# Hybrid encoder step: the overflow experts and the final combination move into the experts' block, and semaphores count from zero

## The reference

```
mod = silu(c) @ w_ada + b_ada                       # six rows of 1024 for each group
h = rms_norm(x, norm_mix) * (1 + sc1) + sh1
m = token_mixer(h, ...)                             # HGRN2 and GLA, chunked recurrences
    # merged = sigmoid(ga) * (o_hg @ w_br_a) + sigmoid(gb) * (o_gla @ w_br_b); m = merged @ w_out
x2 = x + g1 * m
h2 = rms_norm(x2, norm_ffn) * (1 + sc2) + sh2
# 32 experts (4 groups of 8), 2 chosen for each token with weights wts
y = sum over the two chosen experts: wts * ((silu(h2 @ w_gate[e]) * (h2 @ w_up[e])) @ w_down[e])
x3 = x2 + g2 * y
out = rms_norm(x3, norm_final)                      # and the new recurrent states
```

## Time and profile before

| | |
|---|---|
| median of 3 runs | 1918.81 us (1918.67 to 1918.93) |
| the profiled execution | 1918.63 us |
| its span in the profile | 1916.8 us |
| mean granted PE clock | 0.924 |
| busy: PE, DVE, ACT, POOL | 1617.3, 1274.5, 953.3, 323.6 us |
| instructions | 26572 |

### The profile page before, as it was taken

How to read it: one execution, slowest core, us unless ns; L and a number is a source line. 1 busy time by engine, 2 the same in 40 slices (tenths; PEclk the granted TensorE clock), 3 DMA queues, 4 the chain that set the end, 5 groups by cost and what they waited for, 6 DMA issues and landing times. The chain is left out here.

```text
span 1916.8 us, 26572 instructions
## 1 busy us (share of the span) xinstructions
PE 1617.3 (84%) x10704; PEld 1413.7 (74%) x10704; DVE 1274.5 (66%) x1507; ACT 953.3 (50%) x1159; POOL 323.6 (17%) x186
## 2 busy tenths in 40 slices
PE   4579999999899998985696996499999999999800
PEld 2459989988789898984696785388888888887600
DVE  2534368267658575855454436789999999998727
ACT  2724234332625353443102211478888888888623
POOL 0100001000101010100220000134442332322113
PEclk8789999999999999998698998699999999999955
DMA  8722101201111202111542534699999999999546
GB/s 337 292 57 68 35 12 64 88 25 35 60 47 36 70 23 73 34 51 52 182 137 90 201 121 136 234 344 370 377 376 382 378 360 372 367 371 373 200 177 234
DMA packets 189073, 347.06 MB, mean 181 GB/s; under 512 B 18290, under 2 KB 74202, under 8 KB 187868
## 3 DMA queue, kind: packets, MB, share of 16 engines
q1 hardware_dynamic: 171676, 308.48, 45.4%
q10 hardware_dynamic: 7392, 19.06, 2.6%
q0 software_dynamic: 9888, 17.88, 2.5%
HBM read 316.71 MB, written 44.38 MB: 188 GB/s over the span
## 5 line engine op out<-in xcount | busy, mean ns | idle before, releaser
L133 PE MATMUL x_psum_proj<-h_hi,x_w_hi 128*128 128x364 f32 (+1 forms) x1056 | 362.7, 343 | 23.6 <-ACT x_v L652 11.8
L134 PE MATMUL x_psum_proj<-h_lo,x_w_hi 128*128 128x364 f32 (+1 forms) x1056 | 351.3, 333 | 0.0
L135 PE MATMUL x_psum_proj<-h_hi,x_w_lo 128*128 128x364 f32 (+1 forms) x1056 | 351.0, 332 | 0.0
L133 PEld LDWEIGHTS x_psum_proj<-h_hi,x_w_hi 128*128 128x128 f32 x1056 | 202.1, 191 | 32.5 <-ACT x_v L652 12.7
L134 PEld LDWEIGHTS x_psum_proj<-h_lo,x_w_hi 128*128 128x128 f32 x1056 | 202.4, 192 | 2.3
L135 PEld LDWEIGHTS x_psum_proj<-h_hi,x_w_lo 128*128 128x128 f32 x1056 | 202.1, 191 | 0.0
L510 POOL CAST x_w_hi<-x_w 128x1024 fp32r<-128x1024 f32 x44 | 73.1, 1661 | 664.6 <-PE x_psum_proj L135 662.2
L1751 POOL DMA_INDIRECT scratch_y<-e_y,all_tbl x32 | 79.6, 2486 | 392.3 <-ACT e_y L1825 367.8
L1006 DVE TENSOR_REDUCE x_sc<-x_diag 64x64 f32<-64x448 f32 x136 | 126.9, 933 | 1.1
L133 PE MATMUL e_psum_g<-e_g_hi,e_x_hi 128*128 128x512 f32 x256 | 105.9, 414 | 19.3 <-DVE e_x_lo L1901 18.9
L999 DVE TENSOR_TENSOR x_diag<-x_psum_sc,all_shapes 128x448 f32<-128x448 f32 (+1 forms) x72 | 44.6, 620 | 97.8 <-PE x_psum_sc L555 93.9
(11 more groups left out here) (322 smaller groups left out, 3887.2 us busy)
## 6 DMA issues: line engine op xcount, KB each, us to landing
mg_ring_hi<-in_w_e_gate SPq DMA_DIRECT2D x34, 1024.0 KB, 14.3
mg_ring_lo<-in_w_e_down SPq DMA_DIRECT2D x34, 1024.0 KB, 15.1
mg_ring_hi<-in_w_e_up SPq DMA_DIRECT2D x32, 1024.0 KB, 11.9
mg_ring_lo<-in_w_e_up SPq DMA_DIRECT2D x32, 1024.0 KB, 13.6
mg_ring_lo<-in_w_e_gate SPq DMA_DIRECT2D x30, 1024.0 KB, 14.3
mg_ring_hi<-in_w_e_down SPq DMA_DIRECT2D x30, 1024.0 KB, 14.3
c_w<-in_w_ada SPq DMA_DIRECT2D x12, 2048.0 KB, 15.3
x_w<-in_w_in SPq DMA_DIRECT2D x44, 512.0 KB, 3.9
```

Of the source, the lines that this page charges most:

```text
L133: nc.tensor.matmul(out, lhs[0], rhs[0], start=start, stop=False)
L134: nc.tensor.matmul(out, lhs[0], rhs[1], start=False, stop=False)
L135: return nc.tensor.matmul(out, lhs[1], rhs[0], start=False, stop=stop)
```

## The change

Four things change.

1. Semaphores count from zero. `raise_to_start` is called no more, except for the semaphores of the overflow part and only if it runs. Every wait is `reach(eng, sem, n)`, which leaves out a wait for zero.
2. `merge` has no hardware loop: Python writes its 8 pieces out, with constant waits and addresses.
3. `overflow` and `combine` are no stages of their own: they stand behind the experts in the same block, on each engine. The overflow part uses the SBUF of the expert weights and the experts' PSUM, and stands inside an `If(n > 0)`; POOL, SP, ACT, DVE and PE read `n_extra` after their own last expert.
4. The combination: x2 and the rows g2 and norm_final are loaded by SP into ring slots whose halves of the last experts have been subtracted; all 9 tiles of y are loaded at once, when POOL has seen the last scatters land; x2 is added on the DVE instead of POOL; the root is taken for groups of tiles (3, 3, 2 and 1) instead of for each; the output is written over y, so no store has to be waited for.

```diff
+def reach(eng, sem, n):
+    if n > 0:
+        eng.wait_ge(sem, n)
...
         @block.sync                                   # in every stage
         def _(sp):
-            raise_to_start(sp, s)
...
-            with sp.Fori(0, KD // 2) as i:            # merge; the same on the other engines
+            for i in range(KD // 2):
                 for j in range(2):
-                    c0 = sp.snap(i * (2 * P) + j * P)
-                    row_a, row_b = sp.snap(i * 2 + j), sp.snap(i * 2 + j + KD)
-                    sp.wait_ge(w_lo_done, after(2 * i + j - 1))
-                    hold(sp, s)
+                    c0 = i * (2 * P) + j * P
+                    row_a, row_b = i * 2 + j, i * 2 + j + KD
+                    reach(sp, w_lo_done, 2 * i + j - 1)
...
         @block.sync                                   # experts, behind the loads of the weights
+            for part, t in (("g", 0), ("u", NT // 2)):
+                sp.wait_ge(lo_done[part], 2 * NE)
+                sp.dma_start(early["x2_rows"][:, t:t + NT // 2, :],
+                             x2_d[t * P:(t + NT // 2) * P, :].rearrange("(t p) d -> p t d", p=P)).then_inc(x2_in, 16)
+            sp.wait_ge(lo_done["d"], 2 * NE - 2)
+            sp.dma_start(x3[NT][0:T_SAMPLE], x2_d[T_PROMPT:T, :]).then_inc(x2_in, 16)
+            for g in range(2):
+                sp.dma_start(g2[:, g, :], mod_d[g:g + 1, 5 * D:6 * D].partition_broadcast(P)).then_inc(rows_in, 16)
+            sp.dma_start(nf, a["norm_final"].rearrange("(o d) -> o d", o=1).partition_broadcast(P)).then_inc(rows_in, 16)
+            n = number(sp)                            # waits for listed, then reads n_extra
+            with sp.If(n > 0):
...
+            sp.wait_ge(combined, 1)
+            for t in range(NTT):
+                t0, n = TILES[t]
+                sp.dma_start(ys[0:n, t], y_rows[t0:t0 + n]).then_inc(y_in[t], 16)
+            for t in range(NTT):
+                sp.wait_ge(out_ready, t + 1)
+                sp.dma_start(dst, ys[0:n, t, 0, :]).then_inc(out_done, 16)
+            sp.wait_ge(out_done, 16 * NTT)
...
         @block.gpsimd
             scatter(NE - 1)
+            n = number(pool)
+            with pool.If(n > 0):
...
             pool.wait_ge(tabled, NK * 16)
             for b in range(2):
                 pool.wait_ge(y_out[b], arrived(NE // 2 - 1))
+            pool.sem_inc(combined, 1)
...
         @block.scalar                                 # behind keep_y(NE - 1) and its own If(n > 0)
+            scale_y(0)
+            scale_y(1)
+            for t in range(NTT):
+                if t + 2 < NTT:
+                    scale_y(t + 2)
+                square(t)
+                for i, (_, tb) in enumerate(GROUPS):  # GROUPS = [(0, 3), (3, 6), (6, 8), (8, NTT)]
+                    if t + 1 == tb:
+                        root(i)                       # ln and exp on 128 x (tiles of the group)
...
         @block.vector                                 # behind the last low("d", e) and its own If(n > 0)
+            def mixed(t):
+                ...
+                V.scalar_tensor_tensor(out=yt, in0=yt, scalar=wts[0:n, t, 1:2], in1=y1[0:n, t % 3, :],
+                                       op0=ALU.mult, op1=ALU.add).then_inc(y_summed, 1)
+                dve.wait_ge(y_summed, t + 1)
+                V.tensor_tensor(yt, yt, g2[0:n, g, :], ALU.mult).then_inc(y_gated, 1)
+                dve.wait_ge(y_gated, t + 1)
+                V.tensor_tensor(x3[t][0:n], x3[t][0:n], yt, ALU.add).then_inc(x3_ready, 1)
...
+            def normed(i):                            # three small instructions for the group, then its outputs
+                ...
+                for t in range(ta, tb):
+                    V.scalar_tensor_tensor(out=ys[0:n, t, 0, :], in0=x3[t][0:n], scalar=stat[0:n, 5, t:t + 1], in1=nf[0:n],
+                                           op0=ALU.mult, op1=ALU.mult).then_inc(out_ready, 1)
...
+            dve.wait_ge(rows_in, 16 * 3)
+            dve.wait_ge(x2_in, 16 * 3)
+            done = 0
+            for i, (ta, tb) in enumerate(GROUPS):
+                for t in range(done, min(tb + 1, NTT)):
+                    mixed(t)
+                done = min(tb + 1, NTT)
+                normed(i)
...
-        overflow(nc, a, route, *lists)
-        combine(nc, a, scratch["mod"], scratch["x2"], scratch["y"], outs, consts, route)
```

More of the change, by code:

```diff
@@ L338, in _ @@
         def _(pe):
-            pe.wait_ge(ident_ready, after(1))
-            pe.wait_ge(small_in, landed(3))
-            pe.wait_ge(c_dve, after(2))
+            pe.wait_ge(ident_ready, 1)
+            pe.wait_ge(small_in, 48)
+            pe.wait_ge(c_dve, 2)
             for k in range(KD):
@@ L478, in kept @@
         def kept(u, name):
-            return after(place[(u, name), NC - 1] + 1)
+            return (place[(u, name), NC - 1] + 1)
         def out_landed(u, sub):
-            return landed(sum(1 for n in SUB[:u] if n > sub))
+            return 16 * (sum(1 for n in SUB[:u] if n > sub))
         @block.sync
         def _(sp):
-            raise_to_start(sp, s)
             sp.dma_start(lr_w[:, :, :], w_cols[:, :, LR:LR + RANK]).then_inc(lr_in, 16)
@@ L1214, in _ @@
         def _(pe):
-            with pe.Fori(0, KD // 2) as i:
+            for i in range(KD // 2):
                 for j in range(2):
                     n0 = (2 * i + j) * NC
-                    pe.wait_ge(w_lo_done, after(2 * i + j + 1))
+                    reach(pe, w_lo_done, 2 * i + j + 1)
                     for c, (c0, n) in enumerate(COLS):
-                        pe.wait_ge(b_gated, after(n0 + max(c - 1, 0)))
+                        reach(pe, b_gated, n0 + max(c - 1, 0))
                         for half, p_x, done in ((0, p_a, a_done), (K, p_b, b_done)):
@@ new lines, in experts @@
+        v.held = v.sem("held")
+        s.soft += v.sems + v.soft
+        GROUPS = [(0, 3), (3, 6), (6, 8), (8, NTT)]
+        g2, nf, x3 = early["g2"], early["nf"], early["x2"]
+        ys = s.over("ys", "g_hi", 0, [P, NTT, 2, D])
+        y1, junk = s.over("y1", "d_lo", 0, [P, 3, D]), s.over("junk", "d_lo", 12 * D, [P, D])
+        stat = s.sb("stat", [P, 6, NTT])
+        wts = route["wts"]
+        rows_in, x2_in, y_in = s.sem("rows_in"), s.sem("x2_in"), [s.sem(f"y_in{t}") for t in range(NTT)]
@@ L1927, in _ @@
                 low("d", e)
+            n = number(dve)
+            with dve.If(n > 0):
+                dve.wait_ge(v_tbl_in, landed(1))
+                V.tensor_scalar(v_src[:, :], v_tbl[:, :], 1, None, ALU.logical_shift_right).then_inc(v_src_ready, 1)
+                with dve.Fori(0, n) as e:
+                    dve.wait_ge(v_silu_act, after(e * 4 + 3))
+                    V.scalar_tensor_tensor(out=v_act[:, :], in0=p_g[:, :], scalar=0.0, in1=v_act[:, :],
+                                           op0=ALU.min, op1=ALU.subtract).then_inc(v_silu_dve, 1)
+                    dve.wait_ge(v_silu_act, after(e * 4 + 4))
+                    V.tensor_tensor(v_act[:, :], v_act[:, :], p_g[:, :], ALU.mult).then_inc(v_silu_dve, 1)
+                    dve.wait_ge(v_silu_dve, after(e * 2 + 2))
+                    dve.wait_ge(v_u_done, after(e + 1))
+                    V.tensor_tensor(v_act[:, :], v_act[:, :], p_u[:, :], ALU.mult).then_inc(v_hid_ready, 1)
@@ L2303, in program @@
             out_router(nc, a, scratch["mod"], scratch["x2"], scratch["h2"], m_hi, m_lo, ident, consts, route, early)
-            lists = (scratch["table"], scratch["h2"], scratch["y"], ident)
-            experts(nc, a, consts, route, *lists, early)
+            x2_rows = m.over("x2", "hi", 0, [P, NT, D])
+            rest = m.over("rows", "lo", 0, [P, 4, D])
+            early.update(x2=[x2_rows[:, t, :] for t in range(NT)] + [rest[:, 0, :]], x2_rows=x2_rows, g2=rest[:, 1:3, :], nf=rest[:, 3, :])
+            experts(nc, a, scratch["mod"], scratch["x2"], outs, consts, route, scratch["table"], scratch["h2"], scratch["y"], ident, early)
             m.clear()
-        overflow(nc, a, route, *lists)
-        combine(nc, a, scratch["mod"], scratch["x2"], scratch["y"], outs, consts, route)
 OUTPUTS = [(1, T_PROMPT, D), (1, T_SAMPLE, D), (1, 1, HG_HEADS, HG_DK, DV), (1, 1, GLA_HEADS, GLA_DK, DV),
```

844 lines of the change are left out of this document (378 added, 466 removed).

## The result

The changed kernel takes 1876.69 us (median of 4 runs, 1873.25 to 1879.09), the kernel before on the same chip 1918.87 (1918.67 to 1919.62): ratio 0.978, 95% interval 0.976 to 0.980. 1880.5 was predicted, range 1873 to 1890. The two profiled executions have 1918.63 and 1875.61 us, 43.0 apart; the sum of the steps was 38.1.

The account below looks back on a forecast made before the run. The 93.4 us tail was taken as bound by waits first, then by a loop of load, compute and store. Tail 29.5 plus starts 8.6 gave 38.1 off 1918.63: 1880.5 us, range 1873 to 1890.

Parts of the forecast that it names:

- Up to the first scaling: From the last scatter's landing to ACT's first scaling of y: 5.3 us instead of 26.4, 21.1 us gained.
- Rival A: POOL's reading of n_extra and jump over the overflow loop cost up to 3.9 us, all exposed: 1884.4 us; chance 0.12.
- The combination: First scaling to last output: DVE works through nine tiles without waiting, 48.8 us instead of 57.7, 8.9 us gained.
- the Newton step: DVE's step in the combination: 0.75 us each, four times instead of nine, 3.0 us.
- rival E: Loads of y stretch all 36 large DVE instructions, 56.2 us lost against 38.1 gained: 1936.6 us; chance 0.02.
- The early loads: x2 and three rows, issued by 1805, are over by 1820: cost 0, without that cover 14.9 us.
- The end: After the last output, the experts' clear and the ring's clear stand one behind the other: 0.5 us lost.
- The starts: Stages begin without SP's increments: first stage 1.8, mixers 3.6, output projection 2.7, merge 0.5, experts 0; 8.6 us gained.
- the two that I called plain: Mixers and output projection, whose first products wait for SP's loads: all of 3.6 and 2.7 us gained.
- clock, open: Output projection: mean grant 0.76 from 1053 to 1067 lost 3.4 us of work; a shifted start may regain or lose that.
- The experts' start: First product waits for DVE's chain of list instructions, so SP's 1.5 us of increments give 0 (bounds 0 and 1.5).
- what would show it: Signs to check in the trace; the prediction is wrong if, among others, the experts' loop changes length by over 2 us.

Follow-up runs that it names:

- no_branch: The changed kernel without the overflow code, so no engine reads the number of further entries and none jumps: 1876.83 us, ratio 0.980.
- late_loads: The changed kernel with x2 and the three rows loaded only after the last scatter has landed, ahead of the loads of y: 1894.23 us, ratio 0.988.
- increments_back: The changed kernel with SyncE's 32, 54, 19, 47 and 26 semaphore increments put back at the five stage starts: 1886.31 us, ratio 0.984.
- relief_before: The kernel before with expert 8's third weight left out but for a small piece: 1918.04 us, ratio 1.000.
- before_again: The kernel before, unchanged, run once more for a second profile: 1916.05 us.
- front_only: The kernel before with only counts from zero in five stages and the merge written out, overflow and combination as they were: 1909.51 us, ratio 0.997.
- pool_adds: The changed kernel with the nine additions of x2 given back to GpSimd: 1882.27 us, ratio 0.981.

## Why the prediction was right, and where its sizes were off

**Up to the first scaling: right.** 21.1 us predicted, 31.54 - 10.01 = 21.5 in the profiled pair. The load took 4.85 us from issue to scaling where I had 5.3. Rival A is excluded: in no_branch the way to the first scaling is 0.05 us shorter, and no more. Of the Trainium skill's rule on jumps out of the fetched code (page "Runtime: NRT & Kernel Launch", section "Instruction fetch mechanics") nothing is seen here; whether the flight of the scatter hides such a stall or the target was in reach, no run shows.

**The combination: right, 1 us small.** From first scaling to VectorE's end it was 57.71 us and is 47.87: 9.8 instead of 8.9. The mis-sized term is the Newton step: four times 0.58 rather than 0.75 (0.7 us), because I took the old distance, which began with a 0.21 us instruction of another form; 3.72 instead of 3.74 for a tile gives the rest. VectorE waited for nobody, as worked out. Taking over the nine additions costs VectorE nothing on balance because of the turns with GpSimd: with GpSimd's additions the tail is 8.0 us longer, although VectorE has nine instructions fewer. The 2.84 us in the earlier trace rows have the mark of the same turns, an end 1.08 us behind GpSimd's addition. So rival E falls: beside running loads no large instruction took over 1.28.

**The early loads: right.** They were issued from 1780 to 1793, and late_loads prices the cover at 15.9 us.

**The end: right.** From VectorE's end to the span's end 4.19 us before and 4.67 after, 0.5 lost.

**The starts: the two that I called plain are right to 0.1 us.** Fourteen profiles (four with all increments, ten without or with the merge's alone) give means for each stretch:

```
                                       with      without   difference  predicted
first product, mixers                  105.06    99.71     5.35        5.4
from there to the last mixer/merge     929.91    930.98    -1.1        0.5
from there to the output projection    14.27     11.52     2.75        2.7
output projection                      128.09    126.52    1.6         (clock, open)
from there to the last product         644.44    643.51    0.9         0
```

The first and third rows have hardly any scatter (104.5 to 105.6 against 98.9 to 100.7; 14.1 to 14.5 against 11.4 to 11.7): they are the increments. The others scatter as much as they differ. Mixers and merge take 928.6 to 933.3 us without increments, so that up to 1.1 us may be given back there. In the profiled pair they are 0.8 us longer, and so the output projection begins 7.1 us earlier and not 8. The output projection takes 128.8 and 130.2 in two of the four profiles with increments and at most 127.2 in the ten without. I had named the clock there as open, but slower products are not what makes these two long. Here are increments_back, relief_before and the changed kernel, from its first to its last product, with TensorE's busy time behind the window's length:

```profile
1050.80:1179.60 128.80, 122.47 (x600) 98.73 (x600) 63.09 (x100) 26.94 (x47) 0.00 (x0) 0.96 0.42 149
```

```profile
1047.60:1177.80 130.20, 122.99 (x600) 99.24 (x600) 63.10 (x100) 27.28 (x48) 0.00 (x0) 0.96 0.42 148
```

```profile
1041.60:1168.80 127.20, 122.74 (x600) 99.15 (x600) 63.12 (x100) 26.93 (x47) 0.00 (x0) 0.96 0.43 150
```

TensorE is busy as long in each, at the same mean clock; it waits 6.3 and 7.2 us instead of 4.5, most of the difference in one wait for VectorE's part of h2 (3.17 and 3.48 us instead of 1.67, by the timelines). Whether the increments bring that wait stays open, since before_again has them and takes 126.8. The experts' start gives 0, as taken.

**The step that failed** is the last in "what would show it": the experts' loop was to keep its length within 2 us, and from the first expert to the last product it shortened by 5.5 us in the profiled pair. 2.1 of it are the granted clock over the first two experts (before, after, and the changed kernel with late loads, each over two experts; TensorE's busy time stands behind the window's length):

```profile
1222.20:1263.10 40.90, 34.78 (x136) 28.09 (x137) 28.99 (x21) 24.40 (x21) 2.22 (x1) 0.83 0.73 265
```

```profile
1215.60:1254.40 38.80, 32.65 (x136) 26.55 (x137) 29.00 (x20) 24.38 (x21) 2.23 (x1) 0.85 0.76 278
```

```profile
1215.60:1256.50 40.90, 34.79 (x136) 28.07 (x137) 29.02 (x21) 24.44 (x21) 2.23 (x1) 0.83 0.72 261
```

The same 136 products take 2.1 us more in the first and the third, which are different kernels; that goes with the execution. In these two TensorE is busy for 12.3 us at 1.2 GHz, in the second for 7.9; half of the difference, 2.2 us, is lost work. The other 3.4 (559.84 us against 556.41 from the third expert on) are the late weights, which the second profile of the kernel before doesn't have (556.72). The change did not shorten the loop; what failed is the taking of one profile's loop for the kernel's. So the pair's 43.0 is my 38.1, 5.5 of such draws, 1.4 more in the tail, and 2.0 less up to the first expert. Over all profiles the last product comes 9.5 us earlier, and the tail is 31.0 shorter (mean of the three with the old starts and combination, 93.6, against 62.5 to 62.6): 40.5 together, 2.4 above my sum, of which 1.5 is tail and 0.9 front. The changed kernel's 1876.69 lies 3.8 us below the forecast. About 2 of that is the start of the sum: I subtracted from 1918.63, and the kernel before has medians of 1916.1 to 1917.6 in the later runs.

**What stays open.** front_only puts the starts at 5.6 to 7.4 us, with 1 to 2 us lost again in its tail, and increments_back at 11.1; the profiles say 9.5. By the intervals of the ratios, front_only is uncertain by 2 us and increments_back by 5, so they don't contradict each other. The share of the mixers, the merge and the wait in the output projection isn't settled.

## What to carry to other kernels

Read a stretch without work as a list of what each engine does in it: of 31.5 us here only a scatter, a landing and a load were needed, and the rest could go or lie beside the work that follows. Increments on the engine that issues the first load cost what they take where the first product waits for that load (5.35 and 2.75 us here), and nothing at the experts' start, where it waits for something else. And before a difference in a loop is explained, a second profile of the same kernel is due: 5.5 us here were two executions.

## What the runs showed of the hardware

- VectorE and GpSimd take turns for whole instructions, down to 128x3 elements (1.74 instead of 0.16 us). Handing GpSimd an addition of 2.34 us to save one of 1.22 on VectorE lost 0.9 us for each tile (8.0 / 9).
- An fp32 product of 128x128 with 128x512 appears as two rows of TensorE and takes 3.43 / 4 = 0.86 us at the full grant; the weighted sum of a tile by diagonal matrices takes 3.43, where ScalarE's 1.15 and VectorE's 1.28 do it, and gains only by lying beside VectorE.
- GpSimd's drain at the end of the experts' block took 6.84 us in thirteen of the fourteen profiles. In pool_adds it begins with GpSimd's last addition of 2.33 us, over 50 us behind its last scatter, and takes 9.24, so 6.9 behind that addition. In the kernel before the next stage stands behind it; in the changed kernel it lies beside the combination.
- The same kernel varies by 5 to 10 us between executions. The fourteen profiles, of different kernels, place it in the mixers and merge (928.6 to 933.3), the output projection (126.1 to 130.2), the first two experts (38.7 to 40.9) and, in two of fourteen, in weights that come late near the loop's end (556.3 to 556.8 us in the others, 558.4 and 559.8 in these two).
